# The forget gate's bias rows in the second mixer: 128 equal rows written by DMA in place of a matmul and a copy, with head conversions and the value turn at other steps

## The reference, cut to what matters

```
log_f = log_sigmoid(ff + b_f)                      # (B, S, 8 heads)
c = cumsum(log_f, axis=1)                          # running sum over the tokens
s = einsum('bqhd,bkhd->bhqk', q_block, k) * scale
s = s + c_query[..., None] - c_key[:, :, None, :]  # query term, key term
p = masked_softmax(s, key <= query)
out = p @ v
```

## Time and profile before

| | us |
|---|---|
| median of 3 runs | 1684.82 |
| lowest and highest of the 3 | 1684.52, 1685.41 |
| the profiled execution, its own time | 1686.36 |
| span of the profiled execution | 1684.6 |

### The profile page before, as it was taken

One profiled execution on the slowest core, in us unless ns is written; L12 is line 12 of the kernel. 1 busy time (PEld: TensorE's weight loads), 2 busy tenths in 40 slices (PEclk: granted clock), 3 DMA queues, 4 the chain that ended last, 5 costly groups with the idle time before them and its releaser, 6 DMA issues.

```text
span 1684.6 us, 22206 instructions
## 1 busy us (share of the span) xinstructions
PE 1642.8 (98%) x8041; PEld 1357.0 (81%) x8041; DVE 880.2 (52%) x1443; ACT 706.6 (42%) x1179; POOL 166.6 (10%) x249
## 2 busy tenths in 40 slices
PE   8999999999999999999899999999999999999997
PEld 7676788888888888888777888888888788888887
DVE  5544557777743356667756544443227644444233
ACT  4545454444432226667646333323226622333221
POOL 2011000000000032445402000002000200000001
PEclk9999999999999999999999999999999999999999
DMA  5211222232332252121112322333331123232331
GB/s 181 79 45 39 75 88 97 91 99 100 100 100 92 96 127 72 42 64 51 51 61 77 100 89 98 100 99 90 99 101 51 51 100 93 94 100 88 104 108 51
DMA packets 57157, 144.86 MB, mean 86 GB/s; under 512 B 14160, under 2 KB 20976, under 8 KB 57088
## 3 DMA queue, kind: packets, MB, share of 16 engines
q1 hardware_dynamic: 55680, 141.58, 26.6%
q0 software_dynamic: 688, 1.26, 0.4%
q10 hardware_dynamic: 720, 1.10, 0.2%
HBM read 138.67 MB, written 2.10 MB: 84 GB/s over the span
## 4 chain that ended last, share of the span: by engine, by line
PE 91%; DVE 4%; ACT 3%; issue 2%; DMA 0%; POOL 0%; ACTq 0%; DVEq 0%
PE ps L1820 26%; PE ps L1822 26%; PE ps L1821 26%; PE ps L1991 1%; PE ps L2230 1%; PE ps L2245 1%; PE ps L2283 1%; PE ps L2231 1%; PE ps L1927 1%; PE ps L1925 1%; PE ps L1926 1%; PE ps L1981 1%; ACT whi L769 1%; PE ps L2044 0%; PE ps L2376 0%
## 5 line engine op out<-in xcount | busy, mean ns | idle before, releaser
L1820 PE MATMUL ps<-hhi,whi 128*128 128x512 f32 x1400 | 552.8, 395 | 4.8 <-DVE wlo L1233 4.4
L1822 PE MATMUL ps<-hhi,wlo 128*128 128x512 f32 x1400 | 546.4, 390 | 0.0
L1821 PE MATMUL ps<-hlo,whi 128*128 128x512 f32 x1400 | 546.0, 390 | 0.0
L1233 DVE TENSOR_TENSOR wlo<-raw,whi 128x1024 fp32r<-128x1024 f32 x234 | 286.7, 1225 | 468.8 <-ACT whi L769 466.0
L769 ACT ACTIVATE whi<-raw 128x1024 fp32r<-128x1024 f32 x247 | 261.3, 1058 | 559.8 <-PE ps L1822 559.4
L1820 PEld LDWEIGHTS ps<-hhi,whi 128*128 128x128 f32 x1400 | 263.2, 188 | 68.7 <-issue 8.2
L1822 PEld LDWEIGHTS ps<-hhi,wlo 128*128 128x128 f32 x1400 | 263.2, 188 | 55.7
L1821 PEld LDWEIGHTS ps<-hlo,whi 128*128 128x128 f32 x1400 | 263.5, 188 | 53.4 <-issue 1.2
L1820 PE MATMUL ps<-ahi,whi 128*128 128x512 f32 x480 | 186.7, 389 | 0.0
L1821 PE MATMUL ps<-alo,whi 128*128 128x512 f32 x480 | 186.7, 389 | 0.0
L1822 PE MATMUL ps<-ahi,wlo 128*128 128x512 f32 x480 | 186.7, 389 | 0.0
(11 more groups left out here) (345 smaller groups left out, 1888.0 us busy)
## 6 DMA issues: line engine op xcount, KB each, us to landing
raw<-w_up_b SPq DMA_DIRECT2D x88, 512.0 KB, 3.4
raw<-w_up_a SPq DMA_DIRECT2D x44, 512.0 KB, 3.4
raw<-w_in_b SPq DMA_DIRECT2D x23, 512.0 KB, 3.6
raw<-w_in_a SPq DMA_DIRECT2D x19, 512.0 KB, 3.5
raw<-w_down_b SPq DMA_DIRECT2D x16, 512.0 KB, 3.5
raw<-w_out_a SPq DMA_DIRECT2D x8, 512.0 KB, 3.5
raw<-w_down_a SPq DMA_DIRECT2D x8, 512.0 KB, 3.4
raw<-w_out_b SPq DMA_DIRECT2D x8, 512.0 KB, 3.8
```

The source lines that it names most:

```text
L1233: dve.tensor_tensor(wlow(n), raw[n % RAW][:, :], whigh(n).bitcast(f32), ALU.subtract).then_inc(lo_done, 1)
L1820: pe_.matmul(out, wh, hi, start=start, stop=False)
L1821: pe_.matmul(out, wh, lo, start=False, stop=False)
L1822: return pe_.matmul(out, wl, hi, start=False, stop=stop)
```

## The change

1. `ncb` rows come by DMA. After a group's last key swap (`fk{t}`, h = 1) SP issues two more DMAs, one for each head: the source is one row, on one partition, of `csr`, repeated 128 times; the destination is all 128 partitions of `ncb[:, h, :]`, 2 KB each, 256 KB in all. They signal their own semaphores (`GATE_ROW`), on which DVE's reduction of FoX scores now waits. For t > 0 SP waits before them until the group before has done its reductions.
2. The eight `nc` items go: eight matmuls of 128x512 on TensorE and eight copies of 128x512 on ScalarE.
3. `csr` becomes plain float32 of rows 0 to 7, made by one DVE instruction with the factor -8 in it. The ACT copy, the low parts, `esel` and the clearing of `csr` on GpSimd go.
4. Conversions are at other steps: query heads in steps 2 and 4, key heads in steps 5 and 6, one a step. The wait for the hidden layer's product (`B["hid"]`) goes with the new first conversion, `fq0`.
5. The value turn `fv` moves from step 5 to step 3, ahead of `ct` in step 4.

```diff
-            CONV += [(f"fk{t}", h, fks[:, h, 0, :]) for h in range(2)] + [(f"fq{t}", h, fqs[:, h, :]) for h in range(2)]
-            CONV_AT += [nsa_at(t) + 5, nsa_at(t) + 5, nsa_at(t) + 6, nsa_at(t) + 6]
+            CONV += [(f"fq{t}", h, fqs[:, h, :]) for h in range(2)] + [(f"fk{t}", h, fks[:, h, 0, :]) for h in range(2)]
+            CONV_AT += [nsa_at(t) + 2, nsa_at(t) + 4, nsa_at(t) + 5, nsa_at(t) + 6]
...
-            MISC += [(nsa_at(t), "cs", t, 0), (nsa_at(t) + 4, "ct", t, 0), (nsa_at(t) + 5, "fv", t, 0),
-                     (nsa_at(t) + 6, "nc", t, 0), (nsa_at(t) + 7, "nc", t, 1)]
+            MISC += [(nsa_at(t), "cs", t, 0), (nsa_at(t) + 3, "fv", t, 0), (nsa_at(t) + 4, "ct", t, 0)]
...
+            def gate_rows(t):
+
+                sp.wait_ge(B["forget"], 4)
+                if t:
+                    sp.wait_ge(B["m"], 2 * (fox_at(t - 1) + 4))
+                for h in range(2):
+                    n = 2 * t + h
+                    sp.dma_start(ncb[:, h, :], csr[n:n + 1, :].rearrange("a (p c) -> a p c", p=1)
+                                 .broadcast_to([1, P, S])).then_inc(GATE_ROW[h], 16)
...
                             swap(name, h)
+                            if name[:2] == "fk" and h:
+                                gate_rows(int(name[2]))
...
-                if name == "fk0":
+                if name == "fq0":
                     act.wait_ge(B["hid"], 2)
...
-                act.activation(csr[0:8, :], pB[0:8, 2, :], ACT.Copy).then_inc(B["fz_act"], 1)
...
-                            act.activation(ncb[:, h, :], ps[:, 7, :], ACT.Copy, scale=-8.0).then_inc(B["misc_free"], 1)
...
-                dve.tensor_tensor(esel[:, 0:8], ident[:, 0:8], ident[:, 32:40], ALU.add).then_inc(B["forget"], 1)
-                dve.wait_ge(B["fz_act"], 4)
-                dve.tensor_tensor(csr[32:40, :], pB[0:8, 2, :], csr[0:8, :].bitcast(f32), ALU.subtract
-                                  ).then_inc(B["forget"], 1)
+                dve.wait_ge(B["forget"], 3)
+                dve.tensor_scalar(csr[0:8, :], pB[0:8, 2, :], -8.0, None, ALU.mult).then_inc(B["forget"], 1)
...
-                                dve.wait_ge(B["misc_free"], MISC_NO["nc", t, hh] + 1)
+                                dve.wait_ge(GATE_ROW[hh], 16 * (t + 1))
                                 bias, scale = ncb[:, hh, 0:w], -0.125
...
-                    if kind == "nc":
-                        pe_.wait_ge(B["forget"], 5)
-                        n = 2 * t + h
-                        last = pe_.matmul(ps[:, 7, :], esel[:, n:n + 1].broadcast_to([P, P]), csr[:, :],
-                                          start=True, stop=True)
```

More of the change, by code:

```diff
@@ L220, in build @@
         ncb = sb("ncb", [P, 2, S], f32, mb)
-        csr = sb("csr", [P, S], f32r, mb)
-        esel = sb("esel", [P, 32], f32r, mb)
+        csr = sb("csr", [P, S], f32, mb)
         identr = sb("identr", [P, P], f32r, mb)
@@ L287, in build @@
             SWAP = {k: sem("swap_" + k) for k in ("ks", "kw", "fk0", "fk1")}
+            GATE_ROW = [sem(f"b_gate_row{h}") for h in range(2)]
         BANK_MS = 4
@@ L666, in _ @@
                         pool.dma_start(cpe[rows, kv * 32:kv * 32 + 32], pe[kv]).then_inc(ld_cmp, 16)
-                for buf in (kca[:, :, :], kcb[:, :, :], vcs[:, :, :, :], csr[:, :]):
+                for buf in (kca[:, :, :], kcb[:, :, :], vcs[:, :, :, :]):
                     fill(pool.memset(buf.bitcast(f32), 0.0))
@@ L1104, in mix_b @@
                 act.activation(triangr[:, :], triang[:, :], ACT.Copy).then_inc(B["const_r"], 1)
-                act.wait_ge(B["forget"], 3)
-                act.activation(csr[0:8, :], pB[0:8, 2, :], ACT.Copy).then_inc(B["fz_act"], 1)
                 act.preload_act_table(ACT.Gelu_apprx_tanh)
@@ L1173, in mix_b @@
                             values(2 + t, 7, fvs)
-                        if kind == "nc":
-                            if t:
-                                act.wait_ge(B["m"], 2 * (fox_at(t - 1) + 4))
-                            act.activation(ncb[:, h, :], ps[:, 7, :], ACT.Copy, scale=-8.0).then_inc(B["misc_free"], 1)
                     for j, m in enumerate(OUT_ORDER):
```

## The result

The changed kernel takes 1728.91 us (median of 4 runs, 1728.30 to 1729.46) against 1684.91 us (4 runs, 1684.52 to 1685.41). The ratio is 1.0255, with a 95% interval of 1.0241 to 1.0269: 44.0 us slower.

The account below looks back on a forecast made before the run. TensorE, busy 98% of the span, was taken as the bound. Waits for row 0 (27.6), for row 1 (9.6) and lowered clock (6.8), less gains of 6.1, gave +37.9 us on 1684.82: 1723 us, range 1676 to 1748.

Parts of the forecast that it names:

- D: Time of one row DMA's data, all read from one partition: 9.1 to 13.7 us, taken as 10.5.
- Step 8: FoX step 8, each group: TensorE waits for row 0, 6.6 us in groups 0 to 2, 7.8 in group 3; 27.6 together.
- The weight loads: Weight loads issued behind the rows land late, but SP loads three units ahead: cost 0.
- The clock: After each group's long pause the granted clock falls, 1.7 us a time: 6.8 us for four.
- Step 10: Two steps after row 0 is wanted, TensorE waits another 2.4 us a group for row 1: 9.6 us.
- The moves at no cost: Value turn in step 3 and query heads in steps 2 and 4 fall where VectorE has room: 0.
- The gain of 6.1 us: Sum of gains expected from products, group 3's step 5, its clock and small waits: 1.6 + 2.4 + 1.7 + 0.4.
- The seven products: Seven of the eight dropped gate products, 0.23 us each on TensorE's path: 1.6 us gained.
- Group 3's step 5: With one key conversion left ahead of the reductions, TensorE goes on earlier: 2.4 us gained, eighth gate product included.
- the 1.7 us of the clock: Group 3, after step 5: if the shortened pause no longer lowers the clock, 1.7 us come back.
- steps 6 and 7 of groups 1 and 2: For groups 1 and 2 the forecast gave 0.4 us, for small waits on the reductions in step 5.
- the hidden rows: Rival: one-partition reads spread like the swap's, row 0 lands ahead of step 8, gains kept: 1677 us, chance 0.14.

## Why the prediction was right, and where it was not

**The price of a row: right.** D was to lie between 9.1 and 13.7 us, and I took 10.5. 256 KB at the 26 to 29 GB/s of the stretches above are 9.0 to 10.1 us, and row 1 lands 21.7 - 11.8 = 9.9 us after row 0. The reason was half right. I argued from how few partitions are touched and got the pace from an engine that reads at full speed with no gaps. The runs with a second source show the limit to be something that the sources n and n + 32 share and n + 64 does not, the port in the words of the page. That the bounds fitted is luck: the pace that the source allows all 16 DMA engines together, 26 to 29 GB/s, happens to be near what one DMA engine reaches at its best, 459 / 16 = 28.7 GB/s.

**Step 8: right in place, mechanism and size.** VectorE stands 7.83 us in group 0 (forecast 7.8), TensorE's scores come 6.75 us late where 6.6 was forecast, and group 3, without slack, loses 7.9 (7.8). Four groups: 26.9 for 27.6. The weight loads were rightly put at 0.

**The clock: right, and slightly small.** PEclk is at 0.50 behind the pause and step 9 loses 7.7 us where I had 6.8.

**Step 10: wrong.** I charged 2.4 us a group, since row 1 was to land 10.5 us after row 0 and TensorE needs 8.1 for the two steps between. That holds at full clock only, and I had just charged a lowered clock to those same two steps. With its 2.0 us they take 10.1 us in group 0, longer than the 9.9 between the rows; 10.4 were measured (691.85 to 702.28), 0.4 of them the loss of step 10. VectorE waits 1.06 us in group 0 and 0.28 at most later, and TensorE next to nothing. The run with the old steps shows the term as it would be after a shorter pause: where step 9 loses no clock (groups 0 and 2), step 10 loses 2.16 and 1.23 us; where it does, none. The two terms exclude each other in part: 9.6 us were charged and 0.6 came, 9.0 too much.

**The moves at no cost: wrong.** "VectorE has as much room as any step" was said of steps 2 and 4 without a look at their blocks. Step 2 has one. The moves lose 9.0 us in steps 2 to 5, and the run with the moves alone, and the one with the queries in 3 and 4, show that step 2 is the place of most of it. Step 5's key conversion also took 1.7 us in groups 1 to 3, not the 0.7 of the sum, because of GpSimd. The rows had it: the two key conversions of group 3's step 5 took 2.44 us, the two query conversions of step 6 only 1.40, so the first of the pair was no 0.7.

**The gain of 6.1 us: wrong in most terms.** The seven products gave 0.7 us, not 1.6: with the new steps only those of step 6 in groups 0 to 2 count, at 0.2 to 0.3 us each, and with the old steps none does, as the runs with early rows show. The others stood in holes ahead of a reduction. Group 3's step 5 gave 1.3, not 2.4, since the conversion that stayed took 1.72 us; the pause of 1.84 us was still followed by PEclk 0.50 and 0.68, so the 1.7 us of the clock did not come. In steps 6 and 7 of groups 1 and 2 the emptier steps by themselves gave 1.2 us (the moves alone), more than the 0.4 I gave them; what shortened there I did not trace. Together 3.4 us came, for 6.1.

So the total came out within 6 us of the measured one (+37.9 for +44.0, or +42.1 in the traces) by errors on both sides: 9.0 us too much for row 1 and 0.7 for row 0, and against them 9.0 too little for the moves, 2.7 for the gain, 0.9 for the clock and 1.5 behind the last step. That the two errors of 9.0 us cancel is luck; the mechanism of the rows, the wait and the clock is not. Of the rivals, the hidden rows needed D under 2.6 us, and D was 9.9; what it claimed for the rest, 1677 us, also falls, as the version in which the rows are hidden gives 1686.6 with the old steps and 1691.2 with the new, beside 1686.4 and 1686.9 for the kernel before.

**Left open:** why the value turn in step 5 costs step 4 1.35 us in groups 1 to 3 when only the conversions of the kernel before are moved, and nothing with early rows and queries in 3 and 4, why group 0 alone loses 1.1 us in step 5, and the 1.5 us behind the last step. None was tried.

## What to carry to other kernels

Price a broadcast DMA by its source: one partition feeding 128 ran at 26 to 29 GB/s, kept all 16 DMA engines busy for 20 us with 512 KB, and held up what was issued behind it (a swap landed in 7.6 us for 2.3, a weight load in 19.2 for 3.8). Give it a place with nothing urgent behind, or don't use it where a product in a hole costs nothing. When two costs are summed for neighbouring steps, check that the first (a lowered clock, a late start) doesn't use up the time for which the second is charged. And before a small piece is moved "for free", count what the other engines do in just that step: TensorE's blocks there, and GpSimd's instructions beside it.

## What the runs showed that I had not expected

A swap that is issued behind the rows held SP's queue itself for 8.08 us, where one takes 0.46 to 0.60 us alone; in groups 2 and 3 of that run the same issue took 6.28 and 6.19 us. So behind these transfers the issuing queue stood too, not only the landing of what stands behind. And a matmul on the engine that bounds the kernel can be free: with the conversions in their old steps eight of them, on an engine 98% busy, were worth nothing, and the 0.4 us that came were a copy's on ScalarE.
